# Layer C's attention: softmax weights scaled and turned in one product with a diagonal

## The reference, cut to what matters

```
gates = sigmoid(gate_logit)
p_c = masked_softmax(q @ kc * scale, cmp_mask);  o_c = p_c @ vc        # compressed keys
p_s = masked_softmax(q @ k_g * scale, causal);   o_s = p_s @ v_g       # selected keys
p_w = masked_softmax(q @ kw * scale, window);    o_w = p_w @ vw        # window
out = gates[0] * o_c + gates[1] * o_s + gates[2] * o_w
```

## Time and profile before

| | us |
|---|---|
| runs | 2567.61, 2567.74, 2574.58 |
| median | 2567.74 |
| the profiled execution, its own time | 2567.51 |
| its span, first to last instruction | 2566.2 |
| layer C's attention in it | 946 to 1195 |

### The profile page before, as it was taken

The page is one execution under the profiler, slowest core; times in us unless marked ns, Lnnn a source line. Parts: engine busy times, 40 slices in busy tenths (PEclk is TensorE's granted clock), DMA queues, the critical chain, the costliest instruction groups (busy, mean ns, idle before and its releaser), DMA issues.

```text
span 2566.2 us, 29575 instructions
## 1 busy us (share of the span) xinstructions
PE 2326.7 (91%) x10920; PEld 1679.3 (65%) x10920; DVE 1431.4 (56%) x3707; ACT 543.1 (21%) x1325; POOL 65.9 (3%) x67
## 2 busy tenths in 40 slices
PE   8997889999999978889999999999788789888887
PEld 7863578888888864446888888887466533333332
DVE  6549856656666547777765665764766511211114
ACT  2013332100101014443210010201564211211111
POOL 0000000000000000000000000000000011111110
PEclk9998989999999958778999999999899899999998
DMA  5212003222224300001222222223002589999996
GB/s 204 89 50 67 1 17 91 90 82 89 92 82 151 95 4 1 1 1 30 86 83 90 91 82 85 91 88 103 1 1 87 211 321 419 419 419 418 420 420 286
DMA packets 69456, 350.18 MB, mean 136 GB/s; under 512 B 10805, under 2 KB 11061, under 8 KB 43777
## 3 DMA queue, kind: packets, MB, share of 16 engines
q1 hardware_dynamic: 64144, 339.18, 35.6%
q0 software_dynamic: 4880, 8.05, 0.8%
q10 hardware_dynamic: 288, 1.05, 0.1%
HBM read 343.05 MB, written 17.30 MB: 140 GB/s over the span
## 4 chain that ended last, share of the span: by engine, by line
PE 66%; DVE 8%; DMA 8%; ACT 3%; issue 2%; SPq 0%; DVEq 0%; POOLq 0%; ACTq 0%
PE bank L544 24%; DMA w<-in_experts 7%; PE bank L557 6%; PE bank L552 6%; PE bank L547 6%; PE bank L2237 5%; PE bank L2245 3%; PE bank L535 2%; PE bank L804 2%; PE bank L816 1%; PE bank L791 1%; DVE exps L1662 1%; PE bank L746 1%; PE bank L2213 1%; DVE exps L1833 1%
## 5 line engine op out<-in xcount | busy, mean ns | idle before, releaser
L2237 PE MATMUL bank<-w,xT 128*64 128x512 f32 x1024 | 231.9, 599 | 13.6 <-DMA w<-in_experts 12.8
L2400 DVE COPY square<-bank 128x256 f32<-128x256 f32 x32 | 13.6, 425 | 355.5 <-ACT rope L2331 355.5
L2237 PEld LDWEIGHTS bank<-w,xT 128*64 128x64 f32 x1024 | 71.6, 138 | 168.0 <-issue 129.3
L1188 ACT ACTIVATE exps<-exps,small 128x128 f32<-128x128 f32 (+1 forms) x224 | 124.2, 555 | 224.3 <-DVE small L1662 222.9
L544 PE MATMUL bank<-u,ring 128*128 128x256 f32 x608 | 143.6, 379 | 0.0
L1433 DVE TENSOR_TENSOR third<-first,bank 128x256 f32<-128x256 f32 x108 | 45.5, 421 | 175.3 <-PE bank L544 174.6
L2245 PE MATMUL bank<-w,square 128*64 128x512 f32 x512 | 131.5, 661 | 2.1 <-ACT square L2338 2.1
L544 PEld LDWEIGHTS bank<-u,ring 128*128 128x128 f32 x608 | 115.5, 190 | 15.7
L544 PE MATMUL bank<-h,ring 128*128 128x256 f32 x512 | 121.0, 379 | 0.0
L544 PE MATMUL bank<-h_sums,w_sum 128*128 128x256 f32 x512 | 121.0, 379 | 0.0
L544 PE MATMUL bank<-u_mlp_sums,w_sum 128*128 128x256 f32 x480 | 113.4, 379 | 0.0
(11 more groups left out here) (447 smaller groups left out, 4248.4 us busy)
## 6 DMA issues: line engine op xcount, KB each, us to landing
w<-in_experts SPq DMA_DIRECT2D x192, 1024.0 KB, 27.5
ring<-in_dense SPq DMA_DIRECT2D x216, 512.0 KB, 4.3
w<-y_pairs SPq DMA_DIRECT2D x4, 1024.0 KB, 26.7
consts<-in_consts SPq DMA_DIRECT2D x1, 2054.5 KB, 16.5
x<-in_xT SPq DMA_DIRECT2D x4, 512.0 KB, 7.2
cmp_v<-in_cmp_v SPq DMA_DIRECT2D x1, 2048.0 KB, 9.3
cmp_k<-in_cmp_k SPq DMA_DIRECT2D x1, 2048.0 KB, 13.7
h_tokens<-w SPq DMA_DIRECT2D x4, 512.0 KB, 2.9
```

Of the source, the lines that this page charges most:

```text
L1188: act.activation(e, e, ACT.Exp, bias=neg[:, a:a + 1], scale=-1.0, accum_out=total[:, a:a + 1]).then_inc(s[done], 1)
L2237: ins = k.pe.matmul(bank[a * CAP:(a + 1) * CAP, :], xT[:, kk % 4, kk // 4, :], w[:, (2 * (kk % 2) + a) * EH:(2 * (kk % 2) + a + 1) * EH], ...
```

## The change

The scaling of the weights leaves VectorE. VectorE still makes the factor, gate over sum, one column for each head, and signals `c_inv`. ScalarE multiplies the constant identity by this column and so writes a 128x128 diagonal (`act_nsa_diag`), into one of eight slices of the `square` tiles; it does this in step j for item j-2, behind the exps and ahead of the copy of item j-3. TensorE turns the unscaled weights with a product by that diagonal in the place of the transpose with the identity: the product of `e` as stationary operand with the diagonal is the transposed `e` with each query's column scaled.

```diff
@@ signals
-    s.new("c_lg_done", "c_masked", "c_exp_done", "c_scaled", "c_t_done", "c_turned0", "c_turned1", "c_weighed")
+    s.new("c_lg_done", "c_masked", "c_exp_done", "c_scaled", "c_inv", "c_t_done", "c_turned0", "c_turned1", "c_weighed")
@@ buffers
         k.us["c"] = quarters(k.eb, 3)
+        k.diag = [sq[:, P * i:P * (i + 1)] for sq in k.sqp for i in range(4)]
@@ pe_nsa_turn
         for j in range(b + 1):
-            ins = pe.transpose(k.bank[4 + a][:, j * P:(j + 1) * P], e[:, j * P:(j + 1) * P], k.const("ident"))
+            ins = pe.matmul(k.bank[4 + a][:, j * P:(j + 1) * P], e[:, j * P:(j + 1) * P], k.diag[(2 * n + a) % 8], start=True, stop=True)
@@ act_nsa
+        n = step - 2
+        if 0 <= n < len(NSA):
+            act_nsa_diag(k, n)
         n = step - 3
         if 0 <= n < len(NSA):
             act_nsa_turned(k, n)
@@
+def act_nsa_diag(k, n):
+
+    act, s = k.act, k.s
+    neg, total, inv = soft_columns(k, n)
+    act.wait_ge(s["c_inv"], n + 1)
+    for a in range(2):
+        if n >= 4:
+            act.wait_ge(s["c_t_done"], 2 * (n - 4) + a + 1)
+        act.activation(k.diag[(2 * n + a) % 8], k.const("ident"), ACT.Copy, scale=inv[:, a:a + 1]).then_inc(s["c_scaled"], 1)
@@ dve_nsa_scale
     dve.wait_ge(own.sem, own.link(dve.reciprocal(inv, total)))
-    dve.wait_ge(own.sem, own.link(dve.tensor_tensor(inv, inv, k.gt[:, b, 6 * m + 1 + x:6 * m + 6:3], ALU.mult)))
-    for a in range(2):
-        e = k.E[(2 * n + a) % 6][:, 0:P * (b + 1)]
-        dve.tensor_scalar(e, e, inv[:, a:a + 1], None, ALU.mult).then_inc(s["c_scaled"], 1)
+    dve.tensor_tensor(inv, inv, k.gt[:, b, 6 * m + 1 + x:6 * m + 6:3], ALU.mult).then_inc(s["c_inv"], 1)
```

## The result

The changed kernel takes 2602.42 us (median of five executions, 2599.68 to 2614.59) against 2568.86 of the kernel before: ratio 1.0136, interval 1.0123 to 1.0149. It is slower by 34 us. Forecast were 18 us, inside a range to 2616: the direction and the mechanism came out, the size is off by nearly half.

What follows compares the result with a forecast made beforehand. It took layer C's attention to be bound by a loop of three engines, none full, with ScalarE already holding the step read exactly. A period of 32.88 less 30.62 us, eight times, gave +18: 2567.7 to 2586 us, range 2577 to 2596.

Steps and rivals of the forecast that it cites:

- the working's own parts: Attention loop worked out step by step at the high clock: 32.88 us a period against 30.62, +18 us in eight periods.
- Two passes a block: TensorE's turning: each transpose becomes a true f32 product of two passes, 0.112 us each, 0.224 a block.
- Diagonals of 0.40 us: ScalarE's new work: 128 diagonals of 128x128, taken at 396 ns each.
- a pair pushing by 0.61: ScalarE's queue: two diagonals delay what stands behind them by 0.61 us, with bounds of 0.40 and 0.79.
- The queue's order as the new wait: ScalarE runs exps, two diagonals, then the copy; TensorE's next turn waits for that copy and starts 0.14 us behind it.
- The sum over the eight steps: One attention period from turn to turn, steps 0 to 7, at the high clock: 32.88 us.
- Step 0: First step of a period, behind 16 value passes and compressed logits on TensorE: 5.04 us before, 5.11 forecast.
- step 4: One of the eight steps of an attention period, forecast at 4.00 us from turn to turn.
- the clock is now 1.0 for nearly the whole stage: TensorE's granted clock in the attention, 0.78 before, was chosen as 1.0 because the new turning is denser.
- The rival in which the pattern stays whole: The clock keeps its high and low pattern in the attention: +47 us, 2615 us; chance 0.17.
- +2.26 for each of eight periods: Attention period of 32.88 us less the 30.62 read from one period before; eight periods make +18 us.
- the diagonals cost nothing: Rival: diagonals fall into ScalarE's idle time; 28.6 us a period, -16 us, 2551 us; chance 0.06.

Runs made afterwards that it cites:

- e1: Changed kernel with VectorE's factor made ahead of its mask and ScalarE's diagonals ahead of its exps; 2576.46 us, ratio 1.0028 to the kernel before.
- e9: Changed kernel with ScalarE's copy of the turn before placed ahead of the two diagonals, both behind the exps; 2600.73 us, ratio 1.0126.
- e2: Kernel before with the transpose written as a true product with the constant identity; VectorE still scales, no diagonals; 2595.67 us, ratio 1.0109.
- e4: Changed kernel with six unread products of constants behind the logits of step 1 in each period; 2598.99 us, ratio 1.0112.
- e8: Kernel before without VectorE's scaling, so weights enter the values unscaled; stage 236.9 us against 247.1 (whole 17082 us, which says nothing here).
- e3: Kernel before, transposes and scaling kept, with ScalarE also making the diagonals at the changed kernel's place, read by nobody; 2588.29 us, ratio 1.0069.
- e6: e1 with five unread products of constants a period, two ahead of the turn of step 0, three behind step 1's logits; 2578.92 us, ratio 1.0036.
- e7: Changed kernel with eight unread products of constants a period, two ahead of step 0's turn, six behind step 1's logits; 2605.27 us, ratio 1.0154.
- e10: Kernel before with five unread products of constants a period and VectorE's factor made ahead of the mask; 2565.31 us, ratio 0.9993.

## Why the prediction was wrong in size and right in kind

**Where the time went.** From the first turn of period 0 to the first of period 7 the kernel before takes 213.5 us (957.45 to 1171.00), the changed one 244.7 (966.80 to 1211.49), and 242.1 in its second profile. Seven periods at 33.05 are 231.4. So 17.8 us are the working's own parts, and 13.3 (10.7) are stretches at the low clock. What follows the first turn of the last period takes 27.2 us against 22.3: 4.9. In sum 36.0 (33.4), against a difference of the medians of 34. Set against the forecast of 18: the working's own parts came to 22.7, and the low clock, for which it had nothing, to 13.3 (10.7).

**The steps that held.** Two passes a block, 0.112 each: 0.224 a block, and 0.07 more once a turn, between the heads. Diagonals of 0.40 us were 0.386, a pair pushing by 0.61 was 0.59. The queue's order as the new wait, the copy as what the turn waits for, 0.14 behind it. The sum over the eight steps: 32.88 against 33.05. Step 0, which the longer turn ahead of the value products makes 5.28 and not 5.11, is 0.17 of it; step 4 was forecast 0.13 too long, and the other six 0.01 to 0.03 too short each. With the diagonals off the path the same working gave 29.7 for 29.74 (e1), with the copy first 30.9 to 31.0 for 31.05 (e9), with the product alone 30.9 for 31.03 (e2).

**The step that failed** is the choice "that the clock is now 1.0 for nearly the whole stage". It rose only to 0.89 and 0.91, and the low stretches that remain cost 11 to 13 us, for which the sum had nothing. The rival in which the pattern stays whole (+47) was nearly as wrong on the other side. The prediction saw that the turning would be denser, but the compressed logits of 32 columns, behind which it had seen the clock fall, are left as they are by the change, and the clock still falls behind them in five (four) of the seven periods. The change also makes the wait behind them longer, from 3.16 us between two turns to 4.24, of which TensorE is idle for 1.99 in the period shown. That this wait is the cause is not shown, and it can't be the whole of it: in five of the nine falls of the two profiles the clock is low before the wait begins, and e4 filled most of it and kept three falls. The forecast that the clock would rise was right for the mean; how far it would rise was a choice that no row bore out.

**A smaller term** was mis-sized too: +2.26 for each of eight periods. The seven whole ones before average 30.51 us and not the 30.62 of the one that was read, which makes +2.54, and the last costs 4.9, because its last steps ran at the high clock already. That is 22.7 us in place of 18.

**What the parts are worth.** With every period taken at the high clock, from e1, e2 and the changed kernel (start of the stage 11.2 us, seven periods, the tail as profiled): before as measured 247.1; product alone 11.3 + 217.2 + 25.0 = 253.5, so +6 for the second pass when the clock pays for the rest; product and no scaling, diagonals out of the way, 11.2 + 208.2 + 24.9 = 244.3, so the scaling's leaving is worth 9 (e8: 10), with what the factor's earlier place in e1 gives; all of the change 269.8, so the place of diagonals and factor costs 25, of which e9 gives 2.0 us a period, 14 in seven, to the order of ScalarE's calls alone. The low clock adds 10 to 13 to e1, e2 and the changed kernel alike. The second pass (+6), the scaling (-9), the place (+25 to 26) and the low clock (+13) make the 36 us of the first profile. The rival "the diagonals cost nothing" had named the right condition, but not its size: it had 28.6 us a period and 16 us less than the kernel before, and with the diagonals ahead of the exps a period took 29.74 and the whole 7 us more.

**What stays open.** What makes the clock fall in one period and not in the next was not found. Most low stretches start behind the compressed logits, but not all: in e3 two start in step 7, ahead of them, and some in e6, e7 and e10 ahead of the turn of step 0. Moving these logits to another place was not tried. Nor is it known why the clock between 300 and 346 us was 0.65 to 0.70 in some executions and 0.93 to 1.00 in others of kernels that are the same there.

## What to carry to other kernels

An engine that is idle for half of a stage is not free: ask where in its queue the new work lands and who waits for what is behind it. Put it where the engine waits anyway: with factor and diagonals ahead of the exps a period took 29.74 us, with them behind the exps 33.05. When such a loop is worked out step by step from one period, most steps can be held to a few hundredths of a microsecond, but check it against the mean of all periods and against the last one. And where the loop has a stretch at the low clock, price each step at both levels, and ask of the change what it does to the stretch in which the clock falls, not to the mean.

## What the runs showed of the hardware that was not expected

- Products of constants that nobody reads, put into TensorE's waits, made the kernel before faster: the stage 238.0 us against 247.1, clock 0.94 against 0.78, the whole 0.23% faster (0.11 to 0.36). The same five in e1 (clock 0.95), and six and eight in the changed kernel (0.94, 0.96), gained nothing in the whole that is clear of the spread.
- With twice the passes of one line the clock was low for a shorter part of the stage but was not steady: periods of 33.04 and 35.19 us took turns in the second profile, 6.8 us of low clock costing 2.15 us each.
- A true float32 product of 128x128 by 128x128 costs twice a transpose, not more: two passes, 0.112 us apart at the high clock and 0.213 at the low one, against one of 0.109 and 0.214.
- Executions of the same code differed by some 9 us in an earlier attention, far from the place that was changed: between 300 and 346 us the granted clock was 0.65 to 0.70 in six profiles and 0.93 to 1.00 in eight.
